# Eight sample rows of the closing stage over 128 partitions, dealt-out expert rows, and gates in two column groups

## The chip, the cores and the metric

The kernel runs on one core of one Trainium2 chip. The core has five engines with instruction streams of their own: TensorE (PE; its weight loads are shown apart as PEld), VectorE (DVE), ScalarE (ACT), GpSimd (POOL) and SyncE (SP). SP, ACT and POOL also issue DMA transfers, which sixteen DMA engines of the core carry out; "SPq", "ACTq" and "POOLq" stand for those queues. The metric is the time of one execution on the device in microseconds (us), lower is better; three runs of the kernel before gave a median of 693.38 us (692.94 to 696.12).

## What is computed

One inference step of one decoder layer, in float32: 512 prompt tokens with 16 learned meta tokens ahead of them, and 8 sample tokens with a cache and a state of their own. The token mixing runs an mLSTM and a differential attention side by side; then comes a mixture of experts in which every token goes to two of 32 experts, and a last norm. Cut to what matters here:

```
h = rms_norm(x, g);  p = h @ w_in          # columns: mq mk mv mo | mi mf (the gates, 8 columns) | dq dk dv
gates = p[mi, mf] + b_gates;  ig = gates[:4];  lf = log_sigmoid(gates[4:])
x = x + mixer_output(...) @ w_out          # mLSTM heads and attention heads

g_idx = argmax(softmax(h @ w_group + b_group))           # 4 groups
top_v, top_i = top_k(e_logits[g_idx], 2)                 # 8 experts in a group
for e in range(32):
    act = silu(h @ w_gate[e]) * (h @ w_up[e])
    y = y + gates[:, e] * (act @ w_down[e])
x = x + y
y_prompt, y_sample = rms_norm(x, norm_final)             # 512 and 8 rows of 1024
```

## The kernel before

The program is written out by hand for each engine; no scheduler moves anything. Up to the experts, every engine walks through one list, `ORDER`, and does its part of each item; semaphores (`filled`, `freed` for the PSUM banks, others for data) tie the engines together. The tokens stand in five tiles of rows: tiles 0 to 3 hold 128 prompt tokens each, tile `T4` holds the meta tokens in rows 0 to 15 and the 8 sample tokens in rows 32 to 39 (`S0` to `N4`).

**Projections.** The weights `w_in` come in blocks of 512 columns (2 MB each, `load_block`, L546, three buffers in `WS`). The blocks are used in the order dv, dq, dk, mqk, mv, mo. The item `gates` stands after dq: TensorE multiplies the eight gate columns (in `wg`, padded to 36 columns) with all 552 tokens, 512 of them into bank `t` and 40 into bank `p` (L1851). `wg` is loaded by ACT's queue as its first work, in two transfers of 4-element pieces (L973, L974). ACT then adds the biases and takes the log (L994 to L1001), and DVE runs the scans over time (L1400 to L1414).

**Routing.** After the last rows of `w_out` DVE picks groups and experts. The item `rank` counts each token's place within its expert. An expert has 64 slots; two experts make a pair of 128 slots, one in each partition. `place_rows` (L1341 to L1353) makes one-hot rows from the slot numbers: `riota` holds the numbers 0 to 127 and is compared with a token's slot in its pair, and TensorE's `find_rows` (L1817) turns that into the list of tokens by partition, `slot_ids`. This is done for the first three pairs (`EARLY`) first, with the item `rank`, and for the rest in `late_ids` and `late_rows`. The item `order` makes the table of the experts' order (`table_ready`), which lets SP issue the remaining weight loads.

**Experts.** There are 17 turns (`STATIC`), one for each pair and one for rows that didn't fit. A turn gathers the tokens' rows by an indirect DMA of POOL (`fetch`, L905), transposes them on TensorE (`xt`, L2132), scales them on DVE (`rows_in`, L1724, two halves of four k-blocks, one semaphore step after both), multiplies with gate and up weights (`gate_up`, L2140), and with down weights (`down`, L2153), and scatters the result rows to `out_rows` by another indirect DMA (`store`, L915). A slot without a token has an index out of bounds and moves no row. TensorE's order in turn i is gate_up(i), xt(i+1), dn(i-1), and the transposes of the activations. Weights stand in three sets of two experts; gate, up and down of one expert are 1 MB each (L549, L552, L555), and SP reloads a part of a set when `gate_filled`, `gu_filled` or `dn_filled` says that it was used. SP's last of these are the two down loads of the last pair.

**Closing stage.** After the down product of turn 15 SP reads the residual rows back from DRAM (L726, `x_rows`). After the last scatter has landed (`all_out`) it loads each token's two result rows (L749 for `T4`, L752 for the others). Then, for the tiles in the order `T4`, 0, 1, 2, 3 (`LASTLY`): two weighted additions on DVE (L1786), a sum of squares on ACT (L1209), a root on POOL (L806, L808), and `finish` on DVE (L1751), which for tile k comes behind the additions of tile k+1. In `T4` only the eight sample rows count, so these instructions work on 8 partitions of 1024 elements.

## Time and profile before

| | |
|---|---|
| median of three runs | 693.38 us (692.94 to 696.12) |
| the profiled execution, its own time | 703.3 us |
| its span, first to last instruction | 701.5 us |
| PE busy in the span | 611.1 us, 87% |
| PEld, DVE, ACT, POOL busy | 328.6, 279.6, 139.2, 116.4 us |
| moved by DMA | 161.45 MB, mean 230 GB/s |
| granted clock of PE, mean | 0.944 of full speed |

The page's busy shares are averages over stages with different limits. Stages by time from the span's start: projections 0 to 130 us, attention and mLSTM to about 345 us, output projection and routing to 430 us, experts to 667 us, closing stage to the end. A line of the timeline gives start, duration, engine, source line, operation, output and inputs, and in square brackets how long the engine had been idle and what ended that.

### The profile page before, as it was taken

The numbers are of one execution on the slowest core, as the hardware profiler recorded it, in microseconds if no ns is written. First come the engines' busy times: TensorE is split into PE (matmuls) and PEld (weight loads), VectorE is DVE, ScalarE is ACT, GpSimd is POOL, SyncE is SP. The second block draws the span as 40 slices with busy tenths as digits, with TensorE's granted clock in tenths as the row PEclk, the third lists the DMA queues.
The fourth block names the chain that finished last, engine by engine and source line by source line (L and its number), as shares of the span: only waits on it lengthen the run. The fifth ranks groups of instructions, "written<-read, shape, count | busy, mean of one in ns | idle before, by whom it ended". The sixth has DMA issues, their size and how long they took to land.

```text
span 701.5 us, 8557 instructions
## 1 busy us (share of the span) xinstructions
PE 611.1 (87%) x3155; PEld 328.6 (47%) x3155; DVE 279.6 (40%) x615; ACT 139.2 (20%) x405; POOL 116.4 (17%) x195
## 2 busy tenths in 40 slices
PE   4999999899898999999989996999999777999700
PEld 2444344445544555555545482555555443555300
DVE  3320068333333452568788778311212111121146
ACT  3111041233323454401131000110101100101111
POOL 2350016110040110101021201011121110211023
PEclk9999999999999999999999966999999998999965
DMA  9643337823030210041084798899999999999674
GB/s 282 197 142 135 121 102 207 280 83 118 4 106 15 73 48 0 1 121 62 1 327 156 238 407 328 359 419 419 419 420 421 419 422 421 420 420 415 250 262 166
DMA packets 49378, 161.45 MB, mean 230 GB/s; under 512 B 16443, under 2 KB 17772, under 8 KB 36664
## 3 DMA queue, kind: packets, MB, share of 16 engines
q1 hardware_dynamic: 39624, 143.67, 52.8%
q0 software_dynamic: 7488, 17.19, 7.4%
q8 instruction: 26, 0.43, 0.3%
q10 hardware_dynamic: 2224, 0.04, 0.2%
q14 instruction: 16, 0.13, 0.0%
HBM read 150.91 MB, written 19.01 MB: 242 GB/s over the span
## 4 chain that ended last, share of the span: by engine, by line
PE 68%; DMA 12%; SPq 7%; DVE 5%; ACT 3%; issue 2%; another core or an unknown queue 2%; POOL 1%; POOLq 0%; DVEq 0%; ACTq 0%
PE bank L1869 11%; PE bank L1872 11%; PE bank L2090 8%; PE bank_p L2140 6%; PE scores L2153 6%; DMA WS<-in_w_down_e 4%; DMA FT<-in_w_down_e 4%; PE bank_t L2140 4%; PE bank_t L1886 3%; SPq L552 3%; SPq L555 2%; DMA WS<-in_w_in 2%; SPq L549 2%; PE bank L2132 2%
## 5 line engine op out<-in xcount | busy, mean ns | idle before, releaser
L1872 PE MATMUL bank<-WS,XHT 128*128 128x512 f32 x192 | 87.4, 601 | 2.0 <-DMA WS<-in_w_in 1.5
L1869 PE MATMUL bank<-XHT,WS 128*128 128x512 f32 x192 | 85.0, 597 | 1.0 <-PE bank_t L1886 1.0
L1869 PEld LDWEIGHTS bank<-XHT,WS 128*128 128x128 f32 x192 | 35.7, 190 | 43.3 <-issue 43.0
L1872 PEld LDWEIGHTS bank<-WS,XHT 128*128 128x128 f32 x192 | 34.8, 190 | 42.5 <-issue 40.4
L2140 PE MATMUL bank_p<-WS,XHT 128*64 128x256 f32 x288 | 45.5, 391 | 5.7 <-DVE XHT L1724 1.5
L915 POOL DMA_INDIRECT out_rows<-MVA,slot_ids x17 | 17.0, 1001 | 188.1 <-DVE MVA L1741 188.1
L2140 PE MATMUL bank_t<-WS,XHT 128*64 128x256 f32 x288 | 43.0, 381 | 1.5 <-DMA FT<-in_w_up_e 0.8
L2140 PEld LDWEIGHTS bank_p<-WS,XHT 128*64 128x64 f32 x288 | 27.7, 141 | 21.0 <-issue 4.3
L1741 DVE COPY MVA<-scores 128x512 f32<-128x512 f32 x17 | 11.8, 692 | 56.9 <-PE scores L2153 56.9
L806 POOL TENSOR_SCALAR rr<-ss 128x1 f32<-128x1 f32 (+3 forms) x25 | 7.9, 316 | 158.7 <-ACT XHT L1145 46.3
L2140 PEld LDWEIGHTS bank_t<-WS,XHT 128*64 128x64 f32 x288 | 26.3, 137 | 15.6 <-DMA FT<-in_w_up_e 1.2
L1482 DVE TENSOR_TENSOR scores<-scores,maskneg 128x256 f32<-128x256 f32 (+1 forms) x20 | 7.7, 383 | 57.4 <-PE scores L1966 51.7
L2090 PE MATMUL bank<-WS,XHT 128*128 128x512 f32 x64 | 30.4, 623 | 0.0
L2153 PE MATMUL scores<-WS,FT 128*64 128x512 f32 x72 | 24.7, 683 | 5.7 <-DMA WS<-in_w_down_e 4.8
L2090 PE MATMUL bank<-WS,FT 128*128 128x512 f32 x64 | 29.6, 605 | 0.0
L1762 DVE TENSOR_TENSOR MVA<-DVt,bank_p 128x256 f32<-128x256 f32 x9 | 3.8, 421 | 63.1 <-ACT DVt L1186 63.1
L847 POOL DMA_INDIRECT MO<-in_cache_k,pages x16 | 16.3, 1019 | 68.6 <-DVE Sd L1436 52.4
L985 ACT ACTIVATE MVA<-scores 128x512 f32<-128x512 f32 x17 | 10.1, 597 | 87.0 <-PE scores L2153 87.0
L1762 DVE TENSOR_TENSOR MVA<-DVt,bank_t 128x256 f32<-128x256 f32 x8 | 3.4, 421 | 59.2 <-ACT DVt L1186 59.2
L808 POOL TENSOR_TENSOR rr<-rr,neghalf 128x1 f32<-128x1 f32 (+3 forms) x25 | 25.0, 1000 | 2.2
L2132 PE MATMUL bank<-ident,DVt 128*128 128x128 f32 x136 | 20.5, 296 | 5.4 <-DMA DVt<-tok_rows,slot_ids 5.4
L2153 PE MATMUL scores<-WS,MK 128*64 128x512 f32 x72 | 21.9, 598 | 2.7 <-DMA FT<-in_w_down_e 2.7
(427 smaller groups left out, 1022.6 us busy)
## 6 DMA issues: line engine op xcount, KB each, us to landing
WS<-in_w_gate_e SPq DMA_DIRECT2D x16, 1024.0 KB
WS<-in_w_up_e SPq DMA_DIRECT2D x16, 1024.0 KB
WS<-in_w_down_e SPq DMA_DIRECT2D x16, 1024.0 KB
WS<-in_w_in SPq DMA_DIRECT2D x6, 2048.0 KB, 11.8
XHT<-in_w_gate_e SPq DMA_DIRECT2D x10, 1024.0 KB
XHT<-in_w_up_e SPq DMA_DIRECT2D x10, 1024.0 KB
XHT<-in_w_down_e SPq DMA_DIRECT2D x10, 1024.0 KB
FT<-in_w_gate_e SPq DMA_DIRECT2D x6, 1024.0 KB
```

The source lines that it names most:

```text
L549: sp.dma_start(Wgu[w][:, 0], w_gate_e[0, e].rearrange("(p k) n -> p k n", k=KC)).then_inc(gate_in[w // 2], 16)
L552: sp.dma_start(Wgu[w][:, 1], w_up_e[0, e].rearrange("(p k) n -> p k n", k=KC)).then_inc(up_in[w // 2], 16)
L808: pool.tensor_tensor(dst, dst, neghalf[0:dst.shape[0], 0:n], ALU.pow).then_inc(rsq, 1)
L847: pool.indirect_dma_start(dst, None, cache[0].rearrange("n t h d -> (n t) (h d)"), bass.IndirectOffsetOnAxis(ap=pages[:, b * NPAGES + p:b ...
L915: pool.indirect_dma_start(out_rows, bass.IndirectOffsetOnAxis(ap=slot_ids[:, c, 1:2].bitcast(u32), axis=0), YO[s], None, bounds_check=2 * ...
L1869: mm = pe.matmul(PS[r][:, :], w[:, k, 128 * m:128 * (m + 1)], hT[:, k, 0:512], start=(k == 0), stop=(k == KC - 1))
L1872: mm = pe.matmul(PS[r][:, :], hT[:, k, 128 * m:128 * (m + 1)], w[:, k, :], start=(k == 0), stop=(k == KC - 1))
L1886: mm = pe.matmul(PS[r][64 * u:64 * u + N4, 0:256], hT[:, k, 512:TOK], w[:, k, 256 * u:256 * u + 256], start=(k == 0), stop=(k == KC - 1))
L2090: mm = pe.matmul(PS[b][0:n, :], rows[:, k, col(j):col(j) + n], blkslot[(6 + half) % 3][:, first + k, :], start=(k == 0), stop=(k == 3))
L2132: mm = pe.transpose(bank[k // 4][:, 128 * (k % 4):128 * (k % 4) + 128], src[:, k:D:KC], ident[:, :])
L2140: mm = pe.matmul(gu[64 * u:64 * u + 64, DE * g:DE * g + DE], rows[:, k, 64 * u:64 * u + 64], Wgu[w + u][:, g, k, :], start=(k == 0), stop= ...
L2153: mm = pe.matmul(Sps[64 * u:64 * u + 64, 0, 512 * half:512 * half + 512], act_t[:, f, 64 * u:64 * u + 64], Wdn[w + u][:, f, 512 * half:512 ...
```

## The change

1. **Gates.** ACT's two loads of `wg` stand behind the evacuation of the first dq block instead of at the start. TensorE's gates product into bank `t` is made in two column groups: tokens 0 to 255 into partitions 0 to 35, tokens 256 to 511 into partitions 64 to 99. ACT reads the bank in two halves, so it has six evacuations instead of four.
2. **Early rows.** Two constants (`early_rows`, `early_pairs`) are made ahead, with the first logits. In `rank` two instructions fall away, one in the slot numbers and one before `place_rows`. The twelve small instructions behind `table_ready` become `pair_places`, which is called after `rows_of(0)`.
3. **Dealt-out rows.** `riota` no longer holds 0, 1, 2, ... but the numbers by [[32, 4], [1, 8], [8, 4]]: position 32a + 4b + c holds slot 32a + b + 8c. An expert's tokens, which fill its slots from the first, thus stand in other partitions than before.
4. **Halves.** `rows_in` raises its semaphore after each half, and `gate_up` waits for the first half before k-block 0 and for the second before k-block 4.
5. **Closing stage.** The eight sample rows are laid over 128 partitions of 64 elements (16 partitions a row; `spread`). SP loads `norm_final` in that layout with eight transfers (`gfew`), ahead of the residual rows; POOL makes two masks in turn 3 (`few_masks`); TensorE spreads the two weights by one small product in the last turn and sums the squares over a row's 16 partitions by another at the end.

```diff
@@ SP, behind the down product of turn 15
-            for j in range(NTILES):
-                n = nrows(j)
-                sp.dma_start(X[0:n, j, :], x_rows[128 * j:128 * j + n]).then_inc(x_back[j], 16)
+            for b in range(NDEC):
+                sp.dma_start(gfew[16 * b:16 * b + 16], norm_final.rearrange("(s d) -> s d", d=64)).then_inc(gfin_in, 16)
+            sp.dma_start(X[:, T4, 0:64], spread(x_rows, SEQ + S0)).then_inc(x_back[T4], 16)
+            for j in range(NT):
+                sp.dma_start(X[:, j, :], x_rows[128 * j:128 * (j + 1)]).then_inc(x_back[j], 16)
...
-                sp.dma_start(YG[T4][S0:N4, c], src[SEQ + S0:SEQ + N4, c]).then_inc((x_back, y_in)[c][T4], 16)
+                sp.dma_start(YG[T4][:, c, 0:64], spread(out_rows, SECOND * c + SEQ + S0)).then_inc((x_back, y_in)[c][T4], 16)
@@ POOL
-            link(pool.iota(iscr[:, :], [[1, 128]], base=0, channel_multiplier=0))
+            link(pool.iota(iscr[:, :], [[32, 4], [1, 8], [8, 4]], base=0, channel_multiplier=0))
             link(pool.tensor_copy(riota[:, :], iscr[:, :]))
...
                 store(i)
+                if i == 3:
+                    few_masks()
@@ ACT, its first work
-            g = w_in[0].rearrange("(p k) n -> p k n", k=KC)[:, :, W_COLS["gates"]:W_COLS["gates"] + 8]
-            act.wait_ge(wg_zeroed, 1)
-            act.dma_start(wg[:, :, 0:H], g[:, :, 0:H]).then_inc(wg_in, 16)
-            act.dma_start(wg[:, :, 32:32 + H], g[:, :, H:2 * H]).then_inc(wg_in, 16)
...
                 elif kind == "acc":
                     b, m = item[1:]
+                    if (b, m) == ("dq", 1):
+                        g = w_in[0].rearrange("(p k) n -> p k n", k=KC)[:, :, W_COLS["gates"]:W_COLS["gates"] + 8]
+                        act.wait_ge(wg_zeroed, 1)
+                        act.dma_start(wg[:, :, 0:H], g[:, :, 0:H]).then_inc(wg_in, 16)
+                        act.dma_start(wg[:, :, 32:32 + H], g[:, :, H:2 * H]).then_inc(wg_in, 16)
@@ DVE, rank
-                    link(v.scalar_tensor_tensor(early, eidx[:, None, 0:ne].to_broadcast([128, NTILES, ne]), float(SLOTS), early,
-                                                ALU.mult, ALU.add))
-                    link(v.tensor_scalar(early, early, float(-NOROOM), None, ALU.add))
+                    link(v.tensor_tensor(early, early, early_rows[:, None, :].to_broadcast([128, NTILES, ne]), ALU.add))
...
-                    link(v.tensor_scalar(slot_of, slot_of, float(NOROOM), None, ALU.add))
-                    place_rows(first_onehots, piota[:, 0:EARLY])
+                    place_rows(first_onehots, early_pairs[:, :])
@@ DVE, experts
             def rows_in(dst):
                 for half in range(2):
-                    ins = v.tensor_tensor(dst[:, 4 * half:4 * half + 4, :],
...
-                return ins
+                    v.tensor_tensor(dst[:, 4 * half:4 * half + 4, :],
...
+                                    ALU.mult).then_inc(xt_evac, 1)
...
             rows_of(0)
+            pair_places()
             late_ids()
@@ PE, gates
-                    for b, c0, c1_ in (("t", 0, 512), ("p", 512, TOK)):
-                        for k in range(KC):
-                            mm = pe.matmul(PS[b][0:36, 0:c1_ - c0], wg[:, k, :], hT[:, k, c0:c1_],
+                    for k in range(KC):
+                        for u in range(2):
+                            mm = pe.matmul(PS["t"][64 * u:64 * u + 36, 0:256], wg[:, k, :], hT[:, k, 256 * u:256 * u + 256],
                                            start=(k == 0), stop=(k == KC - 1))
-                        mm.then_inc(filled[b], 1)
+                    mm.then_inc(filled["t"], 1)
+                    for k in range(KC):
+                        mm = pe.matmul(PS["p"][0:36, 0:N4], wg[:, k, :], hT[:, k, 512:TOK], start=(k == 0), stop=(k == KC - 1))
+                    mm.then_inc(filled["p"], 1)
@@ PE, experts
                     for k in range(KC):
+                        if g == 0 and k % 4 == 0:
+                            pe.wait_ge(xt_evac, evacuated + (1 if k else 0))
...
+            pe.wait_ge(fsq, 1)
+            pe.matmul(Sps[:, 1, 0:1], alike[:, :], ss[:, 10 + T4:11 + T4], start=True, stop=True).then_inc(few_filled, 1)
```

What stands on the engines at three places, before and in the change. On ACT at the start of the program (`gmix` is the mixing norm's weight, `WS,ss<-XHT` a sum of squares, `DVt` the evacuated dv block), before:

```order
L970 DMA gmix<-in_norm_mix 128x8
L973 DMA wg<-in_w_in 128x8x4
L974 DMA wg<-in_w_in 128x8x4
L977 ACT_TABLE_LOAD
L977 ACTIVATE lam<-ident 128x1
L983 ACTIVATE WS,ss<-XHT 128x1024 x4
```

and in the change:

```order
L995 DMA gmix<-in_norm_mix 128x8
L997 ACT_TABLE_LOAD
L997 ACTIVATE lam<-ident 128x1
L1003 ACTIVATE WS,ss<-XHT 128x1024 x4
L1003 ACTIVATE WS,ss<-XHT 40x1024
L1005 ACTIVATE DVt<-bank 128x512 x4
L1005 ACTIVATE DVt<-bank_t 40x256 x2
L1005 ACTIVATE FT<-bank 128x512
L1031 DMA wg<-in_w_in 128x8x4
L1032 DMA wg<-in_w_in 128x8x4
```

The two `wg` loads have moved behind the first of the four dq evacuations (`FT<-bank`).

On PE around the gates (`bank_t<-WS,XHT` is the small product of the dq block's last tokens, `bank<-XHT,WS` the dk block), before:

```order
L1886 MATMUL bank_t<-WS,XHT 40x256 x16
L1901 MATMUL bank_p<-ident,XHT 128x40 x4
L1851 MATMUL bank_t<-XHT,wg 36x512 x8
L1851 MATMUL bank_p<-XHT,wg 36x40 x8
L1869 MATMUL bank<-XHT,WS 128x512 x32
```

and in the change:

```order
L1924 MATMUL bank_t<-WS,XHT 40x256 x16
L1939 MATMUL bank_p<-ident,XHT 128x40 x4
L1886 MATMUL bank_t<-XHT,wg 36x256 x16
L1890 MATMUL bank_p<-XHT,wg 36x40 x8
L1907 MATMUL bank<-XHT,WS 128x512 x32
```

Eight products of 512 columns have become sixteen of 256; the eight of 40 columns are unchanged.

On SP behind the last down loads (`TE` is the table whose last entry says how many further blocks there are), before:

```order
L555 DMA WS<-in_w_down_e 128x2048
L555 DMA FT<-in_w_down_e 128x2048
L505 TENSOR_LOAD TE
L505 ISA x2
L726 DMA XHT<-x_rows 128x1024 x4
L726 DMA XHT<-x_rows 40x1024
```

and in the change:

```order
L564 DMA WS<-in_w_down_e 128x2048
L564 DMA FT<-in_w_down_e 128x2048
L514 TENSOR_LOAD TE
L514 ISA x2
L734 DMA FT<-in_norm_final 16x64 x8
L735 DMA XHT<-x_rows 128x64
L737 DMA XHT<-x_rows 128x1024 x4
```

Eight small loads and the spread sample rows now stand ahead of the four residual tiles.

## Rows read from the trace of the kernel before

**Rows 1.** The page's 40 slices, mean busy share of the DMA engines in tenths.

```profile
DMA  9643337823030210041084798899999999999674
```

**Rows 2.** The timeline of the opening: start, duration, engine, line, operation.

```profile
2.31 0.63 ACTq L973 DMA_DIRECT2D wg<-in_w_in  x1
...
13.36 7.13 PE L1872 MATMUL bank<-WS,XHT 128*128 128x512 f32 x16 [1.45 <-DMA WS<-in_w_in]
```

**Rows 3.** The page's DMA queues: packets, MB, share of 16 engines' span.

```profile
q0 software_dynamic: 7488, 17.19, 7.4%
...
q10 hardware_dynamic: 2224, 0.04, 0.2%
```

**Rows 4.** The instructions on wg: time from issue to landing of its loads.

```profile
DMA to landing us min/median/max: 14.1/16.9/19.7
```

**Rows 5.** The timeline around the gates on PE.

```profile
81.04 7.03 PE L1851 MATMUL bank_t<-XHT,wg 128*36 128x512 f32 x16 [0.49 <-ACT FT L985]
87.90 0.74 PE L1851 MATMUL bank_p<-XHT,wg 128*36 128x40 f32 x16
...
116.23 3.65 PE L1886 MATMUL bank_t<-WS,XHT 128*40 128x256 f32 x32
```

**Rows 6.** The timeline from the early rows to the second turn.

```profile
416.39 0.17 DVE L1622 TENSOR_SCALAR MO<-MO 128x10 f32<-128x10 f32 x1
...
432.02 1.29 DVE L1724 TENSOR_TENSOR XHT<-bank,gffn 128x512 f32<-128x512 f32 x2
...
433.37 0.69 PE L2140 MATMUL bank_p<-WS,XHT 128*64 128x256 f32 x1 [1.46 <-DVE XHT L1724]
...
442.77 0.42 PE L1817 MATMUL bank_t<-MVA 128*128 128x48 bf16 x10
```

**Rows 7.** Windows: engines' busy us, PEclk, DMA share, GB/s at the line's end.

```profile
58.00:59.00 1.00, 1.00 (x4) 0.47 (x3) 0.00 (x0) 0.00 (x0) 0.00 (x0) 1.00 0.78 293
59.00:60.00 1.00, 1.00 (x3) 0.38 (x2) 0.00 (x0) 0.00 (x0) 0.00 (x0) 1.00 0.00 0
...
645.00:650.00 5.00, 3.79 (x33) 2.65 (x32) 0.41 (x1) 0.59 (x2) 0.98 (x1) 1.00 0.93 388
650.00:655.00 5.00, 3.67 (x32) 2.21 (x32) 0.00 (x0) 0.33 (x1) 0.00 (x0) 1.00 0.73 301
655.00:660.00 5.00, 2.82 (x14) 1.26 (x16) 0.42 (x1) 0.05 (x1) 0.00 (x0) 1.00 0.43 180
660.00:661.00 1.00, 1.00 (x6) 0.24 (x2) 0.13 (x1) 0.13 (x1) 0.00 (x0) 1.00 0.06 25
661.00:662.00 1.00, 0.27 (x2) 0.08 (x1) 0.56 (x1) 0.74 (x2) 0.00 (x0) 1.00 0.21 49
```

**Rows 8.** The timeline from the last turn's products to the last scatter.

```profile
654.24 0.38 PE L2140 MATMUL bank_p<-FT,XHT 128*64 128x256 f32 x1
...
657.18 3.65 PE L2153 MATMUL scores<-XHT,MK 128*64 128x512 f32 x16 [2.56 <-DMA XHT<-in_w_down_e]
...
660.87 2.43 SPq L726 DMA_DIRECT2D XHT<-x_rows  x5
...
662.10 0.61 PE L2153 MATMUL scores<-WS,FT 128*64 128x512 f32 x1 [0.83 <-DMA FT<-in_w_down_e]
```

**Rows 9.** SP's timeline: a small load of the opening.

```profile
23.31 0.43 SPq L569 DMA_DIRECT2D gm<-in_head_norm_m  x1
```

**Rows 10.** The instructions on out_rows, issued from 662 to 664 us: issue to landing.

```profile
DMA to landing us min/median/max: 7.3/7.3/7.3
```

**Rows 11.** The chain that ended last, in order of time: start, duration, what.

```profile
667.32 4.16 DMA out_rows<-MVA,slot_ids
```

**Rows 12.** The timeline of the closing stage.

```profile
678.22 2.61 DVE L1786 SCALAR_TENSOR_TENSOR XHT<-WS,pw,XHT 128x1024 f32<-128x1024 f32 x2 [0.41 <-DMA WS<-out_rows]
...
681.29 1.27 DVE L1751 SCALAR_TENSOR_TENSOR XHT<-XHT,rr,MK 8x1024 f32<-8x1024 f32 x1 [0.47 <-POOL rr L808]
...
682.70 1.59 POOL L808 TENSOR_TENSOR rr<-rr,neghalf 128x1 f32<-128x1 f32 x1
```

More of the change, by code:

```diff
@@ L487, in drained, with spread @@
             eng.wait_ge(freed[b.rstrip("2")], NTH[item, b] + 1)
+        def spread(rows, first):
+            return rows[first:first + NDEC].rearrange("b (s d) -> (b s) d", d=64)
         def reuse(eng, done, turns):
@@ L2133, in rows_out, with gate_up @@
                 return mm
-            def gate_up(gu, rows, w, due):
+            def gate_up(gu, rows, w, due, evacuated):
                 for g, (loaded, done) in enumerate(((gate_in, gate_filled), (up_in, gu_filled))):
```

103 lines of the change are left out of this document (65 added, 38 removed).

## The prediction

> **What bounds the kernel now.** I read the chain that ended last first, then the windows, then the timeline at the places that the change touches. Up to 130 us the chain is almost only TensorE: it starts late, when the first weight block lands [rows 2], and then has hardly a gap, so a product taken off it there is time off the end unless the next wait fills it. From about 421 us on the bound changes: the DMA engines' share is 8 tenths in two slices and then 9 in every slice up to 649 us [rows 1]. So the expert stage ends when its last bytes have come, and it is worth asking how the sixteen engines end. They end unevenly: the share falls from 0.93 to 0.73 to 0.43 in three windows and to 0.06, until the last down load lands at 662.0 us [rows 7, 8]. The idle share of that slope is 5 x (0.07 + 0.27 + 0.57) + 0.94 + 0.79 = 6.3 us: by so much the last engine ends behind the mean one. A burst without indirect rows ends otherwise, from 0.78 to 0.00 within one window [rows 7]. Behind the stage come one scatter (4.16 us [rows 11]), the loads of the results, and DVE, which goes from tile to tile.
>
> **The change part by part.** The sum is against the profiled execution (span 701.5 us, 703.3 us as a whole). That is 9.9 us over the median of 693.38; I carry the difference in us over to the median.
>
> *Start.* The gate columns are 2,224 packets of a queue of their own for 0.2% of 16 engines' span, 1.4 us per engine [rows 3]; their loads land 14.1 and 19.7 us after issue [rows 4], so they run beside the first block, for which TensorE waits until 13.36 us [rows 2]. Some 0.6 to 1.4 us of engine time goes from in front of that block, and ACT is spared two issues (0.63 us for one [rows 2]). I take 1.2 us; ends 0.4 and 2. Loaded at about 57 us, `wg` is due at 80 us: 23 us for what took 19.7 us at worst, so no wait.
>
> *Gates.* The product into bank t takes from 81.04 to 87.90, 6.86 us. Sixteen products of 256 columns in two column groups are what the small block products are: 3.65 us (the trace counts each product twice, as it does the eight of 512 columns) [rows 5]. That is 3.2 us less. The 40-column part stays at its 0.74 us. DVE's scans and the page products begin after the gates and move ahead with them; two more ACT instructions cost 0.2 us beside TensorE. I take 3.2; ends 0 (the stage behind waits for something that didn't move) and 3.3.
>
> *Early rows.* Two DVE instructions fewer on the way to the first gather and to the table: 0.17 us and a link of 0.04 each [rows 6], 0.4 us; the gather then queues behind weight loads, so 0.3 (0 to 0.4). The twelve instructions of `pair_places`, some 0.23 us apart, 2.7 us, now stand behind the first `rows_in` and push the late one-hots back by as much. Their cover is turn 0's gate and up product, 9.4 us from its start at 433.37 to `find_rows` at 442.77 [rows 6]; the late ids' own instructions with 2.7 us more just fill it. I take 0.1 us against, up to 1 if the cover is short.
>
> *Halves.* TensorE starts turn 0 at 433.37, behind both halves, 1.29 us for the two [rows 6]. Half of that goes: 0.65 us. It counts, since the DMA engines are not yet full there [rows 1] and the next gate loads wait for this product. In later turns the rows are ready long before, so nothing.
>
> *Dealt-out rows.* The unevenness of 6.3 us can only come from transfers that aren't the same on every engine, and the indirect ones are those: tokens fill an expert's 64 slots from the first, about 34 of them on average (2 x 536 / 32), and a slot without a token moves nothing. I assume, and no row shows it, that four neighbouring partitions share an engine, as the new pattern presumes. Then an engine's share of an expert went in steps of four rows and now goes in steps of one, and a quarter of the unevenness is left: 4.7 us gained; ends 0 and 6.3. TensorE allows it: it ended the last up product at 654.6 and then waited 2.56 us for a down load at 657.18; the up and gate loads ahead of it move by about as much as that one [rows 8].
>
> By the Trainium skill, page DMA: Bandwidth & Descriptors, section The descriptor swizzle, four neighbouring partitions go to one engine and the pattern comes back after 32; by that the deal is over eight engines, and the sum stays as it is. No row here shows which engine moves which row.
>
> *Closing stage, queue.* Eight small loads stand ahead of the residual rows. One of that kind takes up to 0.43 us of SP [rows 9], so the residual rows move 3 us back, from 660.87 [rows 8] in the old order of time, and reach into the last scatter. A scatter beside them took 7.3 us [rows 10], the last one, mostly behind them, 4.16 [rows 11]. The cost lies between 0 and 3.1; I take 2.0, nearer the loaded row, since 2 MB at about 400 GB/s and 3 us of delay end after the scatter's rows are due.
>
> *Closing stage, DVE.* The sample tile's `finish` of 1.27 us and its wait of 0.47 us stand between tiles 0 and 1 [rows 12]; with 64 elements they shrink to about 0.2 us. That is 1.5 us. But `finish` of tile 0 then comes so early that it waits for its root, which takes 1.59 us beside DVE [rows 12], and the wait before the first of the large additions is for a load and doesn't shrink. I keep 1.1; ends 0.4 and 1.8. The new products and masks lie in idle time of PE and POOL.
>
> **Sum.** 1.2 + 3.2 + 0.3 - 0.1 + 0.65 + 4.7 - 2.0 + 1.1 = 9.05 us. Span 692.4 us, median 693.38 - 9.05 = 684.3 us.
>
> **The rivals.**
>
> *The deal evens nothing out.* The slope is the engines' own, or the last one isn't the one with most rows. For it: no row names an engine. Against: the sharp end of the burst at 59 us. Then 684.3 + 4.7 = 689.0 us.
>
> *The early gains are swallowed.* A wait between 120 and 345 us that hangs on a transfer or on POOL takes the 4.4 us of start and gates. For it: POOL's page gathers and SP's reloads run all that time. Against: each is released by work that moves too. Then 684.3 + 4.4 = 688.7 us.
>
> *Better than taken.* The slope vanishes nearly whole and the residual rows don't disturb the scatter: 684.3 - 1.5 - 2.0 = 680.8 us.
>
> *The dealt rows load slow engines (slower).* The indirect transfers moved 17.19 MB [rows 3], less 32 page gathers of 0.26 MB: 8.8 MB, 0.55 MB or 21 us per engine at 26 GB/s (420 / 16). Where the last rows of a 32-slot block are half empty, an engine has up to half less than that. If the engines that end last are slow ones, and the old layout spared just them, the deal adds up to 10.5 us to them: 684.3 + 4.7 + 10.5 = 699.5 us. It decides from the point where the last engine of the slope is one with fewer rows than the mean. Against it: they weren't slow in the burst that ended at 59 us [rows 7], which had no indirect rows.
>
> The Trainium skill, page DMA: Bandwidth & Descriptors, section Latency and other measured facts, says that DMA engines 7 and 15 are usually slower than the rest, and suspects POOL's descriptor rings. By that rule this rival's time would come out. The trace can't name an engine.
>
> **How the numbers follow.** Forecast 0.60 (681.5 to 687), nothing from the deal 0.13, early gains swallowed 0.10, better 0.11, slow engines 0.06. A measurement of this kernel tells about 0.5% (3.5 us) from no change, that is below 689.9 or above 696.9. The first four all end below 689.9; a mix of two misses (693.4 with both) puts some chance within. Faster 0.88, same 0.06, slower 0.06. The range leaves out slow engines, mixed misses and little below: 680.3 to 689.3 us.
>
> **What would show it.** Right: the first dv product before 12.6 us; the bank t gates product in 3.6 us, and the dk block's start 4 us earlier; the windows' slope before the last down load shrunk to about 2 us, with the landing 8 to 10 us earlier than 662; DVE's small instructions on 128x64. Wrong: the same slope with a landing earlier only by the early gains; a scatter at the end that takes over 7 us; an ACT or DVE wait between 120 and 210 us longer than before by what the gates gave.

## The result, and the profile after

| | before | changed |
|---|---|---|
| median of the runs made together | 696.27 us (692.94 to 699.22, 14 runs) | 691.63 us (688.28 to 695.26, 14 runs) |
| the profiled execution, span | 701.5 us | 693.2 us |
| granted clock of PE, mean | 0.944 | 0.936 |

The ratio is 0.9931 with a 95% interval of 0.991 to 0.9951: 4.8 us faster, where 9.05 us were forecast. Two later comparisons gave 0.992 [0.9888, 0.9953] and 0.9927 [0.9902, 0.9952]. Ratios leave out the executions that lie more than 1.5% above the fastest of their kernel, medians hold all of them, so where the two disagree the ratio counts. The kernel before also ran slower here than in the three runs that the forecast started from (696.27 against 693.38 us), so the median of 691.63 us lies outside the range for two reasons. The ratio on the old base would be 693.38 x 0.9931 = 688.6 us, just within the range and still above the forecast's 687; the gain, not the base, is what has to be explained. Single executions of one kernel differ by up to 12 us, so the difference between two profiles (8.3 us of span) is no measurement of it either.

**The start.** Timeline of the changed kernel, PE in the opening (start, duration, line, operation, idle time before it and what ended that). It answers to [rows 2].

```profile
7.51 3.39 PE L1844 MATMUL scores<-ident,XHT 128*128 128x128 f32 x16 [7.51 <-DVE XHT L1406]
13.17 8.83 PE L1910 MATMUL bank<-WS,XHT 128*128 128x512 f32 x16 [2.27 <-DMA WS<-in_w_in]
21.84 1.04 PE L1844 MATMUL scores<-ident,XHT 128*128 128x128 f32 x8
```

The first dv product starts only 0.19 us earlier (13.36 before) and takes 8.83 us instead of 7.13. The windows of the changed kernel show why (length; busy us of PE, PEld, DVE, ACT, POOL; granted clock; DMA share; GB/s):

```profile
10.00:14.00 4.00, 1.73 (x8) 1.20 (x7) 0.86 (x2) 0.00 (x0) 0.00 (x0) 0.99 1.05 409
14.00:17.30 3.30, 3.30 (x5) 1.35 (x4) 0.70 (x2) 2.05 (x3) 0.73 (x2) 0.50 1.04 292
17.30:20.00 2.70, 2.70 (x7) 1.14 (x6) 2.00 (x4) 1.40 (x4) 1.68 (x4) 1.00 1.05 388
```

From 14.0 to 17.3 us the granted clock was at the lower level, 1.2 GHz (0.50), after TensorE had waited 2.27 us. The first transposes began 1.0 us earlier than before (7.51 against 8.53 us), and TensorE spent nearly all of that waiting longer for the block.

**The gates.** The same view, for [rows 5]:

```profile
82.55 3.65 PE L1886 MATMUL bank_t<-XHT,wg 128*36 128x256 f32 x32 [0.48 <-ACT FT L1005]
86.00 0.74 PE L1890 MATMUL bank_p<-XHT,wg 128*36 128x40 f32 x16
86.67 5.85 PE L1907 MATMUL bank<-XHT,WS 128*128 128x512 f32 x13
```

3.65 us instead of 7.03, as forecast. The product starts 1.5 us later than before, since the start lost them, and the dk block starts 1.9 us earlier.

**The first turn.** For [rows 6]:

```profile
424.87 1.29 DVE L1757 TENSOR_TENSOR XHT<-bank,gffn 128x512 f32<-128x512 f32 x2 [3.21 <-PE bank L2170]
...
425.71 0.69 PE L2180 MATMUL bank_p<-FT,XHT 128*64 128x256 f32 x1
...
435.23 0.42 PE L1852 MATMUL bank_t<-MVA 128*128 128x48 bf16 x10
```

TensorE starts 0.84 us after the rows' scaling began, 1.35 us before: half a microsecond from the halves. `find_rows` comes 9.52 us after the gate product, 9.40 before: the twelve instructions of `pair_places` cost no more than 0.1 us, and their cover held.

**The slope of the DMA engines.** Windows of the changed kernel, for [rows 7]:

```profile
640.00:645.00 5.00, 3.32 (x30) 2.02 (x26) 0.42 (x1) 0.38 (x1) 0.00 (x0) 1.00 1.01 422
645.00:650.00 5.00, 4.70 (x14) 1.76 (x16) 0.00 (x0) 0.00 (x0) 0.00 (x0) 0.66 0.57 238
650.00:655.00 5.00, 4.45 (x22) 1.54 (x18) 0.76 (x2) 0.87 (x2) 0.98 (x1) 1.00 0.13 41
```

Full share up to 645 us, then down within one window; before it sank over four. The last down load landed at 650.1 us, 11.9 us earlier than before, and the idle share of the slope up to there is 2.2 us, 6.3 before; in the ten other profiles with dealt-out rows that give this landing it is 1.9 to 2.2. Before the last down product TensorE now waited 0.55 us for ACT, and for no load. Before the last but one it still waited for its load, and this product took 5.35 us instead of 3.65:

```profile
645.30 5.35 PE L2193 MATMUL scores<-XHT,MK 128*64 128x512 f32 x16 [1.98 <-DMA XHT<-in_w_down_e]
```

The granted clock fell to the lower level (0.50) from 646 to 648 us, behind that wait of 1.98 us (the window above has 0.66 in the mean); before, it stayed at 1.00 behind one of 2.56 us. So 1.7 us of what the steeper slope gave did not reach the scatter in this execution.

**The last scatter.** Timeline of the changed kernel, for [rows 8] and [rows 11]: SP's residual rows, the last scatter (POOL L926), and the first load of the results (L760), which waits for that scatter's landing.

```profile
650.68 3.58 SPq L734 DMA_DIRECT2D FT<-in_norm_final  x8
654.30 0.42 SPq L735 DMA_DIRECT2D XHT<-x_rows  x1
654.76 1.85 SPq L737 DMA_DIRECT2D XHT<-x_rows  x4
656.86 0.97 POOL L926 DMA_INDIRECT out_rows<-MVA,slot_ids  x1 [3.66 <-DVE MVA L1774]
666.29 0.80 SPq L760 DMA_DIRECT2D WS<-out_rows  x2
```

And the same place in the kernel before, beyond [rows 8]:

```profile
667.32 0.97 POOL L915 DMA_INDIRECT out_rows<-MVA,slot_ids  x1 [3.95 <-DVE MVA L1741]
673.13 0.60 SPq L749 DMA_DIRECT2D WS<-out_rows  x2
```

From the issue of the last scatter to the first load of the results it is now 9.43 us; it was 5.81. The scatter was issued 10.5 us earlier than before and the loads come 6.8 us earlier: 3.6 us are lost between the two rows, of which the forecast had counted 2.0. The scatter itself landed 7.8 us after issue, where [rows 11] had 4.16; the one of turn 15, issued at 652.22 ahead of all residual rows, landed after 2.8, where [rows 10] had 7.3. Windows of the changed kernel behind the issue of the last scatter:

```profile
661.00:662.00 1.00, 0.00 (x0) 0.00 (x0) 0.00 (x0) 0.00 (x0) 0.00 (x0) 0.50 0.93 352
662.00:663.00 1.00, 0.00 (x0) 0.00 (x0) 0.00 (x0) 0.00 (x0) 0.00 (x0) 0.50 0.45 172
```

The DMA engines' share is 0.93 or more from 657 to 662 us; the scatter landed at 664.7.

**Closing.** For [rows 12]:

```profile
667.97 0.28 DVE L1822 SCALAR_TENSOR_TENSOR XHT<-WS,FT,XHT 128x64 f32<-128x64 f32 x1 [11.95 <-DMA WS<-out_rows]
670.77 1.28 DVE L1822 SCALAR_TENSOR_TENSOR XHT<-WS,pw,XHT 128x1024 f32<-128x1024 f32 x1 [1.99 <-DMA WS<-out_rows]
673.43 0.28 DVE L1783 SCALAR_TENSOR_TENSOR XHT<-XHT,rr,FT 128x64 f32<-128x64 f32 x1
676.97 1.42 DVE L1783 SCALAR_TENSOR_TENSOR XHT<-XHT,rr,MK 128x512 f32<-128x512 f32 x2 [0.45 <-POOL rr L819]
```

The sample tile's `finish` takes 0.28 us instead of 1.27. Part of what its additions saved turns into a wait of 1.99 us for tile 0's results, and tile 0's `finish` waits for POOL's root, as the forecast said. From the first load of the results to the end of the span it is 26.9 us, 28.4 before.

### The profile page after: what moved, and what is told of

It reads as the page before. It is cut to its first block and busy times, and to the rows that moved or that the text cites. A ratio compares the mean times of both kernels' runs of the same rounds, so it can differ in the third digit from the quotient of the medians.

```text
span 693.2 us, 8615 instructions
## 1 busy us (share of the span) xinstructions
PE 611.5 (88%) x3175; PEld 332.9 (48%) x3175; DVE 276.9 (40%) x616; ACT 138.9 (20%) x408; POOL 116.5 (17%) x200
## 3 DMA queue, kind: packets, MB, share of 16 engines
q10 hardware_dynamic: 2224, 0.04, 0.2%
## 5 line engine op out<-in xcount | busy, mean ns | idle before, releaser
L1910 PE MATMUL bank<-WS,XHT 128*128 128x512 f32 x192 | 89.8, 615 | 2.7 <-DMA WS<-in_w_in 2.3
L2180 PE MATMUL bank_p<-WS,XHT 128*64 128x256 f32 x288 | 47.1, 405 | 5.6 <-DMA WS<-in_w_up_e 2.2
L926 POOL DMA_INDIRECT out_rows<-MVA,slot_ids x17 | 17.0, 1001 | 182.5 <-DVE MVA L1774 182.5
L2180 PEld LDWEIGHTS bank_t<-WS,XHT 128*64 128x64 f32 x288 | 27.3, 137 | 13.1 <-issue 0.3
L2128 PE MATMUL bank<-WS,XHT 128*128 128x512 f32 x64 | 31.9, 649 | 0.0
L1757 DVE TENSOR_TENSOR XHT<-bank,gffn 128x512 f32<-128x512 f32 x34 | 21.9, 686 | 6.9 <-PE bank L2170 6.9
```

The lines of the kernel that those rows point to most:

```text
L926: pool.indirect_dma_start(out_rows, bass.IndirectOffsetOnAxis(ap=slot_ids[:, c, 1:2].bitcast(u32), axis=0), YO[s], None, bounds_check=2 * ...
L1757: v.tensor_tensor(dst[:, 4 * half:4 * half + 4, :], bank[half][:, :].rearrange("p (k t) -> p k t", t=128), gffn[:, 4 * half:4 * half + 4, ...
L1910: mm = pe.matmul(PS[r][:, :], hT[:, k, 128 * m:128 * (m + 1)], w[:, k, :], start=(k == 0), stop=(k == KC - 1))
L2128: mm = pe.matmul(PS[b][0:n, :], rows[:, k, col(j):col(j) + n], blkslot[(6 + half) % 3][:, first + k, :], start=(k == 0), stop=(k == 3))
L2180: mm = pe.matmul(gu[64 * u:64 * u + 64, DE * g:DE * g + DE], rows[:, k, 64 * u:64 * u + 64], Wgu[w + u][:, g, k, :], start=(k == 0), stop= ...
```

## The experiments

In the texts on record "gfew" is the small norm weight in the layout of 64 columns, and "base" is the kernel that the text names. The four runs of a block shared a chip and the runs of the kernel before.

### The changed kernel again, and three single edits

**Unaltered.**

> The changed kernel once more, unaltered, as the base for the three runs beside it and as a second profile. The profile of the change showed the first dv product 8.83 us long at a lower granted clock, the slope of the DMA share after 645 us sharp, and the last scatter landing after 7.8 us. Theory: all three belong to the kernel and come back: product over 8.3 us, slope idle under 3.5 us, scatter over 6.5 us, ratio to the kernel before 0.993. Rival: the stalls of before at 127 and 203 us (ACT 5.9 us, DVE 5.8 us, released by something remote) were chance, and so was part of the 8.3 us of span between the two profiles; then this profile's span lies nearer to 697 than to 693 us.

694.76 us (12 runs; before 701.23), ratio 0.992. The slope and the late scatter came back (9.61 us from the issue of the scatter to the next load); the long first product did not (7.13 us, as in the kernel before):

```profile
13.13 7.13 PE L1910 MATMUL bank<-WS,XHT 128*128 128x512 f32 x16 [1.97 <-DMA WS<-in_w_in]
```

So the start's loss is not fixed in the kernel; the other two readings are.

**The eight small loads, early.**

```diff
             sp.dma_start(gfin, norm_final.partition_broadcast(128)).then_inc(gfin_in, 16)
+            for b in range(NDEC):
+                sp.dma_start(gfew[16 * b:16 * b + 16], norm_final.rearrange("(s d) -> s d", d=64)).then_inc(gfin_in, 16)
...
             sp.wait_ge(dn_filled, LAST[PAIRS - 2] + 1)
-            for b in range(NDEC):
-                sp.dma_start(gfew[16 * b:16 * b + 16], norm_final.rearrange("(s d) -> s d", d=64)).then_inc(gfin_in, 16)
```

> One edit on the changed kernel: the eight small loads of gfew stand behind the load of gfin, at about 440 us, instead of ahead of the residual rows. Theory (the residual rows, 3.6 us later, run beside the last scatter and make it take 7.8 us instead of 4.2): the residual rows start 3.6 us earlier, the last scatter lands in 4.2 to 5.5 us, the time falls by 2.3 to 3.6 us against the changed kernel. Rival (what loads the last scatter is the deal, or the residual rows wherever they stand, since dn(16) too comes earlier): the scatter still takes over 7 us, and the time stays within 1 us.

690.36 us (6 runs), ratio 0.9851 [0.9804, 0.9898]: 4.8 us under the unaltered kernel by the ratios, with an interval from 0.8 to 8.8 (an estimate from the two ratios' own intervals, as for the other differences of ratios below), and 4.4 by the medians. Timeline of this run:

```profile
649.96 1.86 SPq L737 DMA_DIRECT2D XHT<-x_rows  x4
651.12 0.98 POOL L926 DMA_INDIRECT out_rows<-MVA,slot_ids  x1 [14.65 <-DVE MVA L1774]
656.02 0.97 POOL L926 DMA_INDIRECT out_rows<-MVA,slot_ids  x1 [3.92 <-DVE MVA L1774]
661.87 0.79 SPq L760 DMA_DIRECT2D WS<-out_rows  x2
```

5.85 us instead of 9.4 to 9.6. The rival, that the deal or the rows themselves load the scatter, falls.

**The loads of wg at the start again.**

```diff
+            g = w_in[0].rearrange("(p k) n -> p k n", k=KC)[:, :, W_COLS["gates"]:W_COLS["gates"] + 8]
+            act.wait_ge(wg_zeroed, 1)
+            act.dma_start(wg[:, :, 0:H], g[:, :, 0:H]).then_inc(wg_in, 16)
+            act.dma_start(wg[:, :, 32:32 + H], g[:, :, H:2 * H]).then_inc(wg_in, 16)
...
                     b, m = item[1:]
-                    if (b, m) == ("dq", 1):
...
```

> One edit on the changed kernel: ACT's two loads of wg stand at the start again, as in the kernel before. Theory (without them TensorE makes its first transposes 1 us earlier, then waits 2.3 us instead of 1.5 for the first weight block, and its granted clock falls to the lower level in the first dv product): first transposes at 8.5 us, wait about 1.5 us, the dv product 7.1 us, the second token transposes at 20.3 us instead of 21.8, so the time falls by 0.5 to 1.5 us. Rival (the clock fell by chance, and moving the loads saves 0.2 to 1.2 us as forecast): the dv product takes over 8.3 us here too, or about 7.1 in the changed kernel's second profile, and the time rises by 0 to 1.2 us.

694.79 us, ratio 0.9921 [0.989, 0.9952]: no difference from the unaltered kernel. The first product took 8.76 us with a wait of only 1.69 us ahead of it, so the shorter wait does not keep the clock up, against the theory. The rival's mechanism stands (the clock falls by chance). Moving the loads is worth nothing that these times can show. The profiles taken together show a little: the first dv product begins at 13.5 us on average in the six with the loads at the start (13.17 to 13.87) and at 13.1 in the twelve with the loads behind (12.72 to 13.70).

**Rows not dealt out.**

```diff
-            link(pool.iota(iscr[:, :], [[32, 4], [1, 8], [8, 4]], base=0, channel_multiplier=0))
+            link(pool.iota(iscr[:, :], [[1, 128]], base=0, channel_multiplier=0))
             link(pool.tensor_copy(riota[:, :], iscr[:, :]))
```

> One edit on the changed kernel: riota holds 0 to 127 in order again, so the expert rows are not dealt out. Theory (the deal evens the sixteen DMA engines out): the share of the DMA engines falls over some 15 us again behind the last down load instead of over 5, the idle time of the slope grows from about 3 to about 6 us, and the time rises by 2 to 4.7 us. Rival (the deal evens nothing, the sharper slope of the changed kernel's profile is chance): the slope is as sharp as in the changed kernel and the time stays within 1 us.

700.08 us (12 runs), ratio 0.9987 [0.9955, 1.0019]: 4.7 us over the unaltered changed kernel by the ratios, with an interval from 1.5 to 7.9, and 5.3 by the medians. All other parts together were left with about 1 us (-1.3 to 3.2). Its profile fell on its fastest execution (693.26 us), so its span says nothing, but its shape does. The slope is back, beginning before 635 us:

```profile
630.00:635.00 5.00, 4.17 (x33) 2.63 (x31) 0.69 (x1) 0.87 (x2) 0.98 (x1) 1.00 0.95 398
635.00:640.00 5.00, 3.80 (x36) 2.40 (x34) 0.00 (x0) 0.00 (x0) 0.00 (x0) 1.00 0.79 324
640.00:645.00 5.00, 2.75 (x16) 1.20 (x14) 0.42 (x1) 0.38 (x1) 0.00 (x0) 0.82 0.55 229
645.00:650.00 5.00, 4.45 (x18) 1.52 (x16) 0.76 (x2) 0.87 (x2) 0.00 (x0) 0.84 0.08 34
```

### Single parts on the kernel before

**Unaltered, one look.**

> The kernel before, unaltered, for a second profile. Its first profile had two stalls released by something remote, ACT 5.9 us at 127 us and DVE 5.8 us at 203 us, of which no profile of the four changed kernels has one, and a first dv product of 7.13 us. Theory (the stalls were chance): at most one comes back, and at 218 us TensorE is 1.5 to 4 us earlier than in the first profile, which cost that much of the 8.3 us of span between the profiles. Rival (they belong to the old order of the gates): both come back at the same places. The slope behind the last down load should be shallow again: DMA share under 0.8 by 650 us and not near 0 before 660.

702.45 us. The first dv product took 9.0 us here (7.13 in the first profile of the same kernel), so TensorE was 1.9 us later at 20 us; at 218 us it was 0.7 us earlier than in the first profile, so 2.6 us had been made up between. Of the two stalls DVE's at 203 us did not come back, and ACT's did, one evacuation earlier in the list:

```profile
124.12 0.77 ACT L985 ACTIVATE XHT<-bank_t 40x256 f32<-40x256 f32 x2 [5.26 <-remote]
```

The text on record says that no profile of the four changed kernels had one of these stalls; the traces have DVE's in three of them (5.07 us in the kernel's second profile and with the small loads early, 5.02 with wg at the start), and ACT's in the last of these too. Of all eighteen profiles nine have DVE's and six ACT's. So neither profile's distance from the changed kernel's is worth much by itself. The slope was shallow again: DMA shares 0.91, 0.72 and 0.35 in the windows from 645, 650 and 655 us.

**Gates alone** (the gates product and ACT's evacuations as in the change, the loads at the start).

```diff
+                    for k in range(KC):
+                        for u in range(2):
+                            mm = pe.matmul(PS["t"][64 * u:64 * u + 36, 0:256], wg[:, k, :], hT[:, k, 256 * u:256 * u + 256],
+                                           start=(k == 0), stop=(k == KC - 1))
+                    mm.then_inc(filled["t"], 1)
...
```

> The kernel before with one part of the change: the gates product into bank t in two column groups and ACT's six evacuations; the loads of wg stay at the start. Theory (the saving on TensorE stays on the path to the end): product 3.65 instead of 7.03 us, time 3.2 us less, ratio 0.9954. Rival (the stages behind swallow it): product as short, time within 1 us of before.

Product 3.65 us as in the change. 698.93 us (12 runs; before 700.73), ratio 0.9979 [0.9948, 1.001]: 1.5 us, and the interval (-0.7 to 3.6) holds both 3.2 us and nothing.

**Deal alone** (the one line of the fourth run, the other way round).

> The kernel before with one part of the change: riota holds the dealt-out numbers. Theory (the deal evens the DMA engines, whatever else is changed): the slope behind the last down load sharpens, time 4 to 6 us less, ratio 0.993 or lower, the spread of the runs narrower than that of before. Rival (taking the deal away cost 5.3 us only since the last scatter ran beside the late residual rows): ratio above 0.997.

697.32 us, ratio 0.9934 [0.9902, 0.9966]: 4.6 us (2.4 to 6.9), beside the forecast's 4.7; the medians differ by 3.4. The rival falls: the deal needs none of the other parts. The spread did not narrow (691.78 to 702.26). Windows of this run:

```profile
645.00:650.00 5.00, 3.79 (x36) 2.28 (x34) 0.00 (x0) 0.00 (x0) 0.00 (x0) 1.00 1.01 415
650.00:655.00 5.00, 2.88 (x12) 0.99 (x10) 0.42 (x1) 0.39 (x1) 0.00 (x0) 0.78 0.91 383
655.00:660.00 5.00, 4.45 (x20) 1.62 (x18) 0.69 (x1) 0.87 (x2) 0.55 (x1) 0.88 0.32 96
```

**Eight small loads alone** (DVE's wait for `gfin` is raised to count them in, which the excerpt leaves out).

```diff
             sp.wait_ge(dn_filled, LAST[PAIRS - 2] + 1)
+            for b in range(NDEC):
+                sp.dma_start(FT[:, 12 * TOK - 224:12 * TOK - 160][16 * b:16 * b + 16], norm_final.rearrange("(s d) -> s d", d=64)).then_inc(gfin_in, 16)
             for j in range(NTILES):
```

> The kernel before with one cost of the change and nothing else: eight loads of 4 KB ahead of the residual rows on SP's queue, into the free columns of FT; nothing reads them. Theory (3.6 us of SP's time push 2 MB of residual rows into the last scatter, whoever else runs): the last scatter takes 7 to 9 us from issue to landing instead of 4.2, the time is 3 to 5 us more, ratio 1.004 to 1.007. Rival (only a kernel that has its last bytes early and evenly pays this): the scatter takes under 5.5 us and the ratio is within 0.002 of 1.

703.81 us (12 runs), ratio 1.0029 [0.9993, 1.0065]: 2.0 us more, between -0.5 and 4.6, so less than the theory's 3 to 5 and not told from nothing by the time. The timeline is plain, the same stretch as in the change:

```profile
661.32 3.57 SPq L725 DMA_DIRECT2D FT<-in_norm_final  x8
664.94 2.46 SPq L728 DMA_DIRECT2D XHT<-x_rows  x5
667.77 0.97 POOL L917 DMA_INDIRECT out_rows<-MVA,slot_ids  x1 [3.95 <-DVE MVA L1743]
676.67 0.62 SPq L751 DMA_DIRECT2D WS<-out_rows  x2
```

8.90 us from scatter to load, against 5.81 and 5.74 in the two profiles of the unaltered kernel before. So the late scatter needs only the loads' place on SP's queue and nothing else of the change.

### From the early small loads onwards

**That version again.**

> The changed kernel with the eight loads of gfew behind the load of gfin, once more, with more runs, and as the base for the three kernels beside it. Theory: the last scatter lands again under 6 us from issue, ratio to the kernel before 0.985 to 0.988, which is 0.5% below the changed kernel's 0.992. Rival (half of the first ratio was chance; the eight small loads alone cost the kernel before only 2 us): ratio 0.989 to 0.990.

690.51 us (6 runs; before 700.66), ratio 0.9895 [0.9831, 0.9959]; scatter to load 5.97 us. The ratio lies where the rival put it (0.989 to 0.990), and its interval holds the theory's too, so by itself this does not tell them apart.

**Its gates in one column group again** (the gates edit above, the other way round).

> As its base (gfew early), with the gates product again in one column group and ACT's four evacuations. Theory (3.4 us of TensorE's time and what it frees behind it reach the end): time 3.2 us above the base, ratio to before 0.991. Rival (a later stage takes it; two column groups in the kernel before gave only 1.5 us): time within 1 us of the base. In the profile the ACT stall of 5 us ahead of the dk tokens' evacuation at about 125 us should be back if it belongs to the long gates product.

693.50 us (6 runs), ratio 0.9883 [0.982, 0.9946]. The medians differ by 3.0 us, which hangs on single executions (the slowest took 699.26 us); by the ratios the version with the old product is no slower (0.9883 against 0.9895). So no gain of the gates shows in this comparison. In the two profiles the 3.4 us of the product stay visible behind it: the dk block starts at 88.33 us against 84.84, and ACT's instructions come 4.1 to 4.9 us later from 124 to 350 us and 5.6 to 9.1 later from there to 640, more than the product can account for. ACT's stall did not come back, while it stood in the run with the dealt rows alone (5.30 us), which has the old gates, and in the one with wg at the start (5.17 us), which has the new: the gates do not decide it. It stands in five of the six profiles with the loads of wg at the start and in one of the twelve with them behind; why stays open, and the time with wg at the start shows nothing of it.

**Residual rows of tiles 2 and 3 behind the results.**

```diff
-            for j in range(NT):
+            for j in range(2):
                 sp.dma_start(X[:, j, :], x_rows[128 * j:128 * (j + 1)]).then_inc(x_back[j], 16)
...
                     sp.dma_start(YG[j][:, c], src[128 * j:128 * (j + 1), c]).then_inc((x_back, y_in)[c][j], 16)
+                if j + 1 >= 2 and j + 1 < NT:
+                    sp.dma_start(X[:, j + 1, :], x_rows[128 * (j + 1):128 * (j + 2)]).then_inc(x_back[j + 1], 16)
```

> As its base (gfew early), with the residual rows of tiles 2 and 3 loaded behind the result rows of tiles 1 and 2 instead of ahead of the last scatter. Theory (what the last scatter pays is the megabytes beside it, 2 MB): with 1 MB beside it it lands in 4 to 4.8 us instead of 5.9, and DVE, which takes 4 us for a tile, never waits for the late rows: time 1 to 1.5 us less. Rival (the scatter waits for its own writes, not for bandwidth, or DVE waits for tile 2's rows): time the same or up to 2 us more.

690.85 us (6 runs), ratio 0.9864 [0.9817, 0.9911], level with its base. DVE did not wait for the late rows, but the last scatter took no less: 659.12 to 665.19 us, 6.07. In its base, too, the issue of the residual rows ends 4 us ahead of the scatter, so there was nothing left for halving them to win. Here the DMA engines had fallen idle when it was issued, as the window behind its issue shows, and it still landed after 4.4 us, as it did with the 2 MB four microseconds ahead of it: so much it takes by itself.

```profile
659.00:660.00 1.00, 0.00 (x0) 0.00 (x0) 0.00 (x0) 0.00 (x0) 0.88 (x1) 1.00 0.00 0
```

That less in front does help is seen one scatter earlier, where the 1 MB stands right ahead of it:

```profile
653.32 0.91 SPq L737 DMA_DIRECT2D XHT<-x_rows  x2
654.48 0.97 POOL L928 DMA_INDIRECT out_rows<-MVA,slot_ids  x1 [15.81 <-DVE MVA L1776]
```

This scatter of turn 15 landed after 4.5 us. With the 2 MB of all four tiles issued around it, it took 7.0 to 8.0 us in eleven profiles (7.3 in [rows 10], 7.4 and 7.5 in two of the version that this one starts from), and with none of them around it 2.8 in six. So the theory's mechanism stands and its forecast falls: on the last scatter there was no cost left to halve. A last scatter with 1 MB right ahead of it was not run.

**TensorE kept busy in the opening.**

```diff
                         pe.wait_ge(ident_made, 1)
+                        for _ in range(9):
+                            pe.matmul(PS["a0"][:, 0:128], ident[:, :], ident[:, :], start=True, stop=True)
                     pe.wait_ge(hn_ready, j + 1)
...
+                    if (b, m) == ("dv", 0):
+                        for _ in range(10):
+                            pe.matmul(PS[r][:, 0:128], ident[:, :], ident[:, :], start=True, stop=True)
                     if m == 0 and kind != "post":
```

> As its base (gfew early), with 19 idle products of TensorE on the identity matrix, nine ahead of the first transposes and ten between them and the first dv product. In ten profiles the granted clock rose to its upper level either at 11 to 12 us, and then the first dv product took 7.1 us (four), or at 17 to 18 us or after a fall at 13.9, and then it took 8.8 (the others, before and changed kernels alike). Theory (TensorE's idle time ahead of the product decides, by chance of when it falls): with the engine kept busy the product takes 7.1 us in the profile, time 0.5 to 1.7 us below the base. Rival (the clock does not follow this work, or the idle products push the transposes back): 8.8 us again, time the same or more.

686.61 us (6 runs), ratio 0.983 [0.9769, 0.9891]. Timeline of this run, PE:

```profile
3.29 4.21 PE L1879 MATMUL bank<-ident 128*128 128x128 f32 x18 [3.29 <-POOLq L795]
7.55 2.63 PE L1844 MATMUL scores<-ident,XHT 128*128 128x128 f32 x16
10.02 2.40 PE L1903 MATMUL bank<-ident 128*128 128x128 f32 x20
12.93 7.13 PE L1915 MATMUL bank<-WS,XHT 128*128 128x512 f32 x16 [0.52 <-DMA WS<-in_w_in]
```

The transposes took 2.63 us instead of 3.4 to 3.65, and the product 7.13.

### Four versions side by side

**The changed kernel.**

> The changed kernel beside the three below, on the same chip, so that they can be set against it and not only against the kernel before. Theory: ratio 0.992 to 0.993 again, last scatter over 8.5 us to the next load.

690.89 us (12 runs; before 695.10), ratio 0.9927 [0.9902, 0.9952]; scatter to load 9.67 us.

**Small loads early.**

> The version with gfew early, as the base beside the three others. Theory: ratio 0.985 to 0.989, 2.5 to 4 us below the changed kernel; last scatter under 6 us to the next load.

686.05 us (4 runs), ratio 0.987 [0.9844, 0.9895]; scatter to load 6.04 us. That is 4.0 us (1.5 to 6.4; 0.6%) under the changed kernel by the ratios.

**Small loads early, and TensorE kept busy.**

> The version with gfew early and 19 idle products, once more: its first ratio, 0.983 with an interval of 0.6% either way, is from six runs. Theory (gfew early gives 3 to 4 us, the kept-up clock 0.5 to 2.5 us): ratio 0.983 to 0.988, 4 to 6 us below the changed kernel beside it, first transposes in 2.6 us and first dv product in 7.1 us again. Rival (the first figure was luck): ratio 0.988 or more, dv product 8.8 us.

685.57 us (4 runs), ratio 0.9872 [0.9846, 0.9898]: level with the version without the idle products, though its profile shows 2.63 us for the transposes and 7.13 for the product again, and the version without them 9.00 us for the product. The first figure of 0.983 was luck for the most part, as the rival had it for the time; what the clock gives back in the opening is under what these runs can tell.

**The change without its closing part** (parts 1 to 4 stand; part 5 as before).

> The changed kernel without its closing part: the sample tile on 8 partitions of 1024 elements as before, no gfew loads, no masks, no spreading products; the other four parts stand. Against the version with gfew early it shows what the new layout itself is worth, against the changed kernel what the whole part was worth with its queue cost. Theory (layout +1.1 us, queue -3 to -4 us): 1 us above the version with gfew early, ratio 0.987 to 0.990, and 2 to 3 us below the changed kernel: the closing part as made is a loss. Rival (the layout gives as much as the queue costs): level with the changed kernel, ratio 0.992.

687.80 us (5 runs), ratio 0.9888 [0.9862, 0.9913]. By the ratios that is 2.7 us under the changed kernel (0.2 to 5.2) and 1.3 us over the version with the small loads early (-1.3 to 3.8). So the closing part as made is a loss, narrowly beyond the noise: its eight loads cost 4.0 us where the change put them. What the new layout itself gives, 1.3 us here, is not told from nothing by the times. First load of the results to the end of the span: 28.0 us, and 27.3 in the version with the small loads early.

## Why the prediction was wrong

The direction, the mechanism of the deal and the place of the cost were right; the sum was too large by about 4 us. By its own steps:

- **Dealt-out rows**, 4.7 us: right. 4.6 us alone, 4.7 us taken away. Of the 6.3 us of unevenness 2.2 are left, a third rather than the quarter; that four partitions share an engine was assumed, and what the runs show is that this pattern works, not why. The rival that the deal evens nothing, and the one with slow engines, are out.
- **The queue of the closing stage**, -2.0 us: mis-sized. It measured 3.6 us in the timelines and 4.0 to 4.8 us in the times (2.0 in the kernel before, with an interval from -0.5 to 4.6). The delay was a little short: 3 us were taken, and the eight loads took SP 3.58 (0.45 each, and eight of the 0.43 of [rows 9] would have been 3.4). The step that failed is "I take 2.0", between 0 and 3.1: the late scatter landed after 7.2 to 8.0 us in six profiles, which is the loaded row of 7.3 itself and a little over, and not a value between it and the quiet one. The reason given, that the 2 MB end after the scatter's rows are due, is what the windows show: the engines' share is 0.93 or more until 662 us, where the scatter issued at 656.86 was due at 661.0 by the quiet row; it landed at 664.7. That reason spoke for the whole of the loaded row, and nothing spoke for a part of it. The forecast's own sign of being wrong, a scatter at the end of over 7 us, came true.
- **Start**, +1.2 us: failed in size. The first block's product began 0.2 us earlier in the profile, 0.4 us on average over all eighteen, and not before 12.6 us in any of them; with the loads put back the time did not change. The step "some 0.6 to 1.4 us of engine time goes from in front of that block" took all the 2,224 small packets as work ahead of the block; 0.4 us of it shows. That ACT is spared two issues brought the first transposes forward by 1.0 us, and the wait for the block took it. In the profile the term even turned over to -1.5 us, by the clock. That is chance, not the change: the first product took 7.13 us in one profile of the kernel before and 9.0 us in the other, and 7.13, 7.13 and 8.83 us in the three of the changed kernel.
- **Gates**, +3.2 us: right on TensorE (3.38 us less), and the profiles carry it to the end; in the times it is 1.5 us with an interval from -0.7 to 3.6, and taking it away from the version with the small loads early cost nothing (ratios 0.9883 and 0.9895). The dk block began 1.9 us earlier, not the 4 that the forecast named, since the start had lost its part. How much of it arrives stays open.
- **Early rows and halves**, +0.3, -0.1 and +0.65 us: seen as 0.5 us and 0.1 us in the first turn, not run alone.
- **Closing DVE**, +1.1 us: in keeping with 0.7 to 1.5 us by the timelines; the times give 1.3 us, from -1.3 to 3.8.
- **TensorE's clock behind the last waits**: in no term of the sum. The last but one down product took 5.2 to 5.35 us in ten of the eighteen profiles, the changed kernel's three among them, and 3.65 in the other eight, among them all four of the kernel before without dealt-out rows. It stands on the way to the last scatter. No run takes it by itself, so whether the earlier end of the loads brings it about or chance does is not shown.

With 0.4 for the start and 4.0 for the queue the sum is 9.05 - 0.8 - 2.0 = 6.25 us; 4.8 to 5.6 us were measured. The rest can be the gates, or that clock. The rival "early gains swallowed" described the start rightly and for the wrong reason: what was missing of it was never there. The other part of the miss is the base: 693.38 us was the median of three runs, and the same kernel gave 695.1, 696.3, 700.7 and 701.2 in the comparisons after.

The best version found is the change with its eight small loads behind the load of `gfin`: 0.987 [0.9844, 0.9895] of the kernel before beside a ratio of 0.9927 for the change, and 0.9851 and 0.9895 in two other comparisons. The versions with the idle products (0.9872 beside it) and without the closing part (0.9888) are not told apart from it.

## What to carry to other kernels

When the last thing before the end is an indirect scatter, look at what the queues issue just ahead of it: small loads that nobody waits for can push a large load into it, and whatever is not needed by then belongs in an earlier idle stretch of the queue. Where all transfers are equal but one kind is sparse, deal the sparse rows out; read the DMA share's slope ahead of the last landing to see what that can give. And where a trace holds the loaded case as a row, take that row for the term, not a value halfway to the quiet one.

## What the runs showed of the hardware

- TensorE's granted clock in the opening differs between executions of the same kernel. In the sixteen profiles without idle products, the first dv product took 7.13 us in seven and 8.6 to 9.2 us in nine, before and changed kernels alike. Idle products on the identity matrix from 3.3 us on gave 7.13 us in both profiles that had them. In the time this was not to be told from nothing.
- The last scatter behaved in two ways, with nothing between. In twelve profiles the issue of the residual rows ended 3.8 us or more ahead of it, and it took 4.9 to 6.1 us from its issue to the next load (landing after 3.3 to 4.4 us). In six their issue ended 0.2 to 0.5 us ahead of it, and it took 8.9 to 9.7 us (landing after 7.2 to 8.0). No run puts the rows between these two places.
- The scatter of turn 15 landed after 2.8 us ahead of all residual rows (six profiles), after 4.5 with 1 MB of them right ahead of it (one), and after 7.0 to 8.0 among the 2 MB (eleven). So an indirect scatter pays for the bytes just in front of it, and more for more of them. Whether it waits for them or shares the engines with them these runs do not tell.
- TensorE's granted clock also fell late: 5.2 to 5.35 us for a product that took 3.65 elsewhere, in ten of eighteen profiles. In the changed kernel's profile it fell behind a wait of 1.98 us, in the kernel before it held at 1.00 behind 2.56 us.
- Which rows of an indirect transfer stand in which partitions is worth 4.6 to 4.7 us here by the ratios, 0.7% of the kernel, with the same bytes and the same number of rows.
